# Group A's weighing in 512-column products, once in four steps, in an encoder block kernel

## The reference

```
sc = jnp.einsum('bqkgd,bskd->bkgqs', qblk, k, preferred_element_type=jnp.float32) * scale
p = jax.nn.softmax(sc, axis=-1).astype(v.dtype)
return jnp.einsum('bkgqs,bskd->bqkgd', p, v)
```

## Time and profile before

| | |
|---|---|
| median of 3 runs | 2183.95 us (2181.45 to 2187.36) |
| profiled execution | 2184.07 us |
| its span in the trace | 2182.3 us |
| PE, DVE, ACT, POOL busy | 2109.1, 1536.6, 747.1, 326.3 us |
| mean granted clock of PE | 0.988 of full |
| group A's attention | about 337 to 600 us |
| group B's attention | about 600 to 750 us |

### The profile page before, as it was taken

How to read it: one execution, slowest core, us unless ns; L and a number is a source line. 1 busy time by engine, 2 the same in 40 slices (tenths; PEclk the granted TensorE clock), 3 DMA queues, 4 the chain that set the end, 5 groups by cost and what they waited for, 6 DMA issues and landing times.

```text
span 2182.3 us, 29405 instructions
## 1 busy us (share of the span) xinstructions
PE 2109.1 (97%) x10566; PEld 1706.9 (78%) x10566; DVE 1536.6 (70%) x1985; ACT 747.1 (34%) x1197; POOL 326.3 (15%) x202
## 2 busy tenths in 40 slices
PE   7999999999989999999999999999999999998996
PEld 5778887776777788888888888888888888876885
DVE  7898635777666766677777777777777677767546
ACT  6323114666666721322222221122222221145223
POOL 5222101000011144201001000001001000015101
PEclk9999999999999999999999999999999999998998
DMA  5224357101267330011001001010001001011103
GB/s 178 108 95 154 121 176 173 29 14 29 43 155 165 82 131 32 20 39 39 29 29 38 29 29 38 29 33 34 29 34 33 29 29 38 29 46 41 39 29 116
DMA packets 54459, 139.98 MB, mean 64 GB/s; under 512 B 23296, under 2 KB 23680, under 8 KB 54400
## 3 DMA queue, kind: packets, MB, share of 16 engines
q1 hardware_dynamic: 53536, 138.07, 20.9%
q10 hardware_dynamic: 864, 1.13, 0.1%
HBM read 107.72 MB, written 31.46 MB: 64 GB/s over the span
## 4 chain that ended last, share of the span: by engine, by line
PE 86%; DVE 6%; DMA 2%; ACT 2%; issue 2%; POOL 1%; SPq 1%; DVEq 0%; ACTq 0%; POOLq 0%
PE ps L306 24%; PE ps L308 23%; PE ps L307 23%; PE ps L1160 4%; PE ps L1131 3%; PE ps L1114 2%; PE ps L1115 2%; DMA KLB<-qkl 1%; PE ps L1177 1%; DVE qstd L711 1%; PE ps L1124 1%; PE ps L1097 1%; PE ps L1080 1%; PE ps L1145 1%; DVE NL L1978 1%
## 5 line engine op out<-in xcount | busy, mean ns | idle before, releaser
L306 PE MATMUL ps<-NH,WH 128*128 128x512 f32 x1896 | 746.0, 393 | 21.2 <-DVE WL L694 10.0
L307 PE MATMUL ps<-NL,WH 128*128 128x512 f32 x1896 | 741.8, 391 | 0.0
L308 PE MATMUL ps<-NH,WL 128*128 128x512 f32 x1896 | 741.3, 391 | 0.0
L306 PEld LDWEIGHTS ps<-NH,WH 128*128 128x128 f32 x1896 | 358.3, 189 | 102.9 <-DVE NL L688 16.3
L308 PEld LDWEIGHTS ps<-NH,WL 128*128 128x128 f32 x1896 | 358.4, 189 | 75.3
L307 PEld LDWEIGHTS ps<-NL,WH 128*128 128x128 f32 x1896 | 358.6, 189 | 73.6
L1912 DVE TENSOR_TENSOR H<-H,ps 128x512 f32<-128x512 f32 x480 | 305.5, 684 | 100.9 <-PE ps L308 100.9
L283 POOL TENSOR_TENSOR raw<-raw,gains 128x1024 f32<-128x1024 f32 x76 | 154.2, 2031 | 1164.8 <-DMA raw<-in_w 1164.8
L298 ACT ACTIVATE WH<-raw 128x1024 fp32r<-128x1024 f32 x102 | 107.8, 1057 | 563.7 <-PE ps L308 536.0
L306 PE MATMUL ps<-MH,WH 128*128 128x512 f32 x504 | 196.6, 390 | 0.0
L307 PE MATMUL ps<-ML,WH 128*128 128x512 f32 x504 | 196.4, 390 | 0.0
(11 more groups left out here) (188 smaller groups left out, 2424.5 us busy)
## 6 DMA issues: line engine op xcount, KB each, us to landing
raw<-in_w SPq DMA_DIRECT2D x102, 512.0 KB, 3.3
xst<-in_xT SPq DMA_DIRECT2D x24, 256.0 KB, 3.3
H<-in_xT SPq DMA_DIRECT2D x8, 768.0 KB, 10.0
out_yT<-H SPq DMA_DIRECT2D x24, 256.0 KB, 2.1
Q<-qkh SPq DMA_DIRECT2D x12, 384.0 KB, 6.7
qkh<-oqh SPq DMA_DIRECT2D x5, 768.0 KB, 3.3
qkl<-oql SPq DMA_DIRECT2D x5, 768.0 KB, 4.9
qkh<-obh SPq DMA_DIRECT2D x5, 768.0 KB, 4.8
```

What stands on the lines that cost most here:

```text
L306: nc.tensor.matmul(out, wh, xh, start=first, stop=False)
L307: nc.tensor.matmul(out, wh, xl, start=False, stop=False)
L308: return nc.tensor.matmul(out, wl, xh, start=False, stop=last)
```

## The change

`weigh` of group A is now called once a block, at m = 4b+5, for all four items: 4 or 8 matmuls of 512 columns in place of twice as many of 256. The call at m = 4b+3 is gone, and with it PE goes from the transposes of that step straight to `norm_row`. The waits of `weigh` stay (`t_free` of item 4b+3, `o_sum` of the block before). `PA` has two slots of 512 queries, 32 KB, taken by `(m // 4 + 1) % 2`. `VF` and `PF` move within the region that they share with `PA`, and `VF`'s blocks lie in reverse order. No instruction of DVE, ACT, POOL or SP is added, removed or moved.

```
-        PA = c("PA", [2, TS // P, 2 * P])
-        PF = nc.alloc_sbuf_tensor_at("PF", [P, 2, 3, 2 * P], F32, offset=probs_home)
-        lows_home = c.at
-        VF = c("VF", [VBLOCKS, len(NA_LEFT), P])
-        c = Region(lows_home + 16 * KB)
+        PA = c("PA", [2, TS // P, GT])
+        VF = nc.alloc_sbuf_tensor_at("VF", [P, VBLOCKS, len(NA_LEFT), P], F32, offset=probs_home + 14 * KB)
+        PF = nc.alloc_sbuf_tensor_at("PF", [P, 2, 3, 2 * P], F32, offset=probs_home + 26 * KB)
...
-            return t[:, (m // 2) % 2, n0 * b:n0 * b + n, cols(m % 2, P)]
+            return t[:, (m // 4 + 1) % 2, n0 * b:n0 * b + n, cols(m % 4, P)]
...
-            return flat(VF[:, block, :, :]), ps[:, VBANK, :]
+            return flat(VF[:, VBLOCKS - 1 - block, :, :]), ps[:, VBANK, :]
...
-            def weigh(kind, p, b, m, queries):
+            def weigh(p, b):
 
                 s = b // 3
-                k0, w = window(kind, m)
-                at = (m % 4) * P
-                pe.wait_ge(t_free[0], fills(kind, p, ("T", m + queries // P - 1)) + T_FREE)
-                pe.wait_ge(t_free[1], fills(kind, p, ("T", m + queries // P - 1)) + T_FREE)
+                m = 4 * b
+                k0, w = window("A", m)
+                for half in range(2):
+                    pe.wait_ge(t_free[half], fills("A", p, ("T", m + 3)) + T_FREE)
                 at_least(pe, o_sum, p * 6 + b)
                 todo = places(w)
-                c0 = (m % 2) * P
                 for kb, kn, n in todo:
-                    mm = nc.tensor.matmul(ps[cols(kb % 2, DH), PVBANK, at:at + queries], VA[s][0:kn, k0 // P + kb, :],
-                                          PA[0:kn, (m // 2) % 2, n, c0:c0 + queries],
+                    mm = nc.tensor.matmul(ps[cols(kb % 2, DH), PVBANK, :], VA[s][0:kn, k0 // P + kb, :], PA[0:kn, (b + 1) % 2, n, :],
                                           start=kb < 2, stop=kb >= todo[-1][0] - 1)
-                return mm
+                mm.then_inc(pv_done, 1)
...
-                if kind == "A" and m % 2 == 1:
-                    mm = weigh(kind, p, (m - 3) // 4, m - 3, 2 * P)
-                    if m % 4 == 1:
-                        mm.then_inc(pv_done, 1)
+                if kind == "A" and m % 4 == 1:
+                    weigh(p, (m - 5) // 4)
```

More of the change, by code:

```diff
@@ L1176, in weigh_both @@
                     for half in range(2):
-                        mm = nc.tensor.matmul(ps[cols(half, DH), PVBANK_B[b % 2], cols((m // 2) % 2, P)], VF[0:kn, first + kb, (m + half) % 4, cols(s, DH)],
+                        mm = nc.tensor.matmul(ps[cols(half, DH), PVBANK_B[b % 2], cols((m // 2) % 2, P)], VF[0:kn, VBLOCKS - 1 - (first + kb), (m + half) % 4, cols(s, DH)],
                                               PF[0:kn, (m // 2) % 2, kb, cols(half, P)],
```

## The result

The changed kernel takes 2204.82 us (median of 4 runs, 2202.45 to 2205.66) against 2184.4 in the same comparison: a ratio of 1.0093, 95% interval 1.008 to 1.0106, or 20.4 us more. Its profiled execution has a span of 2202.2 us. The loss lies where the change is. Windows of the changed kernel (stretch, its length, busy us of each engine, clock, DMA): two laps of twelve steps, then the whole stage of group A.

A forecast was written before the change was run, and what follows sets the result against it. The prediction took PE to bound the kernel now, and after the change a ring over PE, DVE and ACT; 2184.1 + 14.1 (eight laps) + 2 (squares) = 2200 us, range 2188 to 2210, with 0.8.

The forecast's parts named there:

- Term 1: PE's bursts in group A: fewer, wider products, a sample burst 3.62 us, a prompt one 1.89, saving 0 to 7.4.
- The estimate of 8 us: PE's bursts: about 60 cycles of overhead per matmul, so 320 records fewer at 25 ns save 8 us, ending at 2192.
- gain of 7.4 us for entries and exits: PE's bursts: one entry (0.17 us) and one exit (0.14) fewer in each of 24 blocks.
- Term 2: PE's wait for DVE's `osum`, with weight loads, goes in group A: 6.7 us at most.
- the ring: Group A: exposed chain over PE, DVE and ACT from one burst's start to the next; +14.1 us, chance 0.76.
- Term 3: Group A: the dropped burst covered DVE's extra 1.50 us; without it a lap takes 33.25 us against 31.49, +14.1 in all.
- The three rings: One lap: sample burst with prompt copy 12.43 us; prompt burst, else samples 10.96; sample burst with prompt scores 9.86.
- Term 4: ACT's queue: squares between an exponential and a copy that PE waits for; 2 us taken, bounds 0 and 6.6.
- A: Attention stage of group A: PE stays the bound, the burst and `osum` gains count, 14.1 us less, 2170 us; chance 0.08.
- B: Group A: gains and losses cancel within 0.3%, 8 to 12 of the 16 us go, 2188 us; chance 0.08.
- C: PE's clock drops through idle pieces of up to 1 us, mean 0.9, 2215 us; chance 0.06.
- D: PE's two column halves no longer run side by side at 512 columns, 70 us more, 2270 us; chance 0.02.

The follow-up runs named there:

- narrow_once: Changed kernel with its one burst in step 4b+5 made of 256-column products again, two sets one behind the other: 2202.7 us, ratio 1.009.
- the wide kernel: Changed kernel with DVE's sum and product two steps later and POOL's first group B bias table ahead of the last pair's first addition: 2179.53 us, ratio 0.998.
- the narrow one: Kernel before, 256-column bursts kept, with DVE's product at the end of step 4b+7, norm rows at 4b+6 and POOL's table moved: 2177.91 us, ratio 0.9969.
- norm_later: Changed kernel with group A's norm rows one step later, behind the transposes of step 4b+4: 2205.19 us, ratio 1.0098.
- wide_small: Changed kernel with DVE's sum of the two halves made for only 8 of 512 columns, so its output is wrong: 2189.15 us, 15.7 less.
- narrow_small: Kernel before with DVE's sum of the two halves made for only 8 of 512 columns, so its output is wrong: 2175.76 us, 8.5 less.
- wide_late: Changed kernel with DVE's sum and product two steps later, end of step 4b+8, norm rows at 4b+7, squares behind the product: 2182.59 us, ratio 0.9997.
- wide_squares: Changed kernel with ACT's squares of group A beside a burst, ahead of the copy of the upper half: 2201.1 us, ratio 1.0094.

## Why the prediction was right

The forecast was 2200, the range 2188 to 2210, the measured time 2204.82. Step by step:

- Term 1, the burst. Forecast: 3.62 us for a sample block, 1.89 for a prompt one. The trace: 3.59 (468.05 to 471.64) and 1.87 (388.76 to 390.63), and twice as many records of half the width take 3.60 in `narrow_once`. The estimate of 8 us from the Trainium skill, "TensorEngine Tiling (Array Packing)", section "Instruction Overhead", finds no support here: 32 records or 16, the time of the burst is one. The estimate also took each record for a matmul; a product leaves two records, so that 160 products went, and by the same figure of the page the estimate would be 4 us.
- Its gain of 7.4 us for entries and exits is shown by no run. PE's busy time in 24 steps went from 61.47 to 61.36 us; with cover it is 60.04 in the wide kernel and 60.70 in the narrow one, 0.66 less, or 2.6 in the stage. None of it shortens a lap: even with cover the wide kernel has the narrow one's (61.31 and 61.22), with PE idle 1.27 us of it where the narrow one has 0.52. The forecast took nothing off for this gain, so the error did no harm.
- Term 2. The wait for `osum` went, as said, and was worth nothing, since it was inside the ring.
- Term 3, the ring, is borne out by four runs: `norm_later` (no single wait), `wide_small` and `narrow_small` (the same work exposed or half covered), `wide_late` (cover given back, loss gone). Its size was put too low: 33.25 us a lap against 34.05 measured. The three rings were forecast at 12.43, 10.96 and 9.86 us. By the starts of the bursts, 388.76, 399.96, 410.61, 423.38, 434.39, 444.50 and 456.86, they took 12.57, 11.11 and 10.38 on average. The first two are within the 0.25 that I allowed a ring; the third is not. One term failed in it in every lap, "row minimum to copy 0.60": it was read from a step whose copied item is a prompt one, and here the copy waits for eight transposes of a sample item, 472.40 to 473.28, 0.88 us. In the lap without squares that is nearly the whole error: its third ring took 10.11 us and its three rings 33.48, 0.23 above the forecast. The lap of the second head took 34.62, 1.37 above. 0.35 of it are squares (34.27 in `wide_squares`). Most of the rest goes with the longer hand-overs at DVE in that head's read-outs: copy to reciprocal 0.72, reciprocal to sum 0.20 and product to row minimum 0.72, against 0.61, 0.08 and 0.60 in the other lap. The sum of the earlier trace rows was read from a read-out of the first head alone and stood for all.
- Term 3 said that a burst hid DVE's extra 1.50 us before the change. It hid only a part: `narrow_small` shows that about half of the sum was on the path. The forecast did not suffer from it, since it set the ring against the measured lap, in which that part is contained.
- Term 4, the squares: 2 us taken, 1.4 measured. One is to be seen in the chain above, between the exponential's end and a copy: the scores started 0.05 us after the exponential, but the transposes had to wait until 478.10 for the copy behind the square.
- So 16.1 us were forecast and 20.4 came. The laps account for it: 14.1 forecast for eight of them, 8 x 0.80 = 6.4 more measured, together 20.5; the squares, for which I had put 2 us apart, are already in these laps. So the mechanism and the sign were right, and the size was four fifths of what came. The forecast's own range has a slip: with the ring's 6 us and the upper end of term 4 it reaches to 2211, not 2209; the measured time lies inside either.
- The rivals. A (PE stays the bound, 2170) and B (2188) were wrong. PE was idle 6.74 of 68.10 us, 10%, where I had 12%. C: the granted clock was 1.00 in the laps and 0.99 in the stage, as before, with idle pieces of up to 1.4 us at L1143; the rule of the Trainium skill, "TensorE: Matmul & The Clock Gate", section "A second HAM failure mode: psum-queue depth-cycling", did not come into play here. D: the bursts streamed at their old pace.

## What to carry to other kernels

An instruction on the engine that bounds is also the cover of what other engines do meanwhile. Before two bursts are merged into one, follow the queue of the engine that waits for them, from the end of one burst to the start of the next, and add up the chain; if it is longer than what is left on the bounding engine, the merger costs the difference. And the largest wait in the table need not be a bound: removing it may only move the idle time to the next link. To gain, move the work on the late engine, here a sum and a product, to just before or beside the burst, and look at what else waits in the queues that the move passes.

## What the runs showed of the hardware

That 16 records of 512 columns and 32 of 256 take the same 3.59 and 3.60 us, with 64 columns of weights in two halves side by side, was not expected to be so exact. Nor was it that DVE's starts follow each other by 0.20 and 0.72 us in the read-outs of the second head and by 0.08 and 0.60 in those of the first, in both kernels, for a cause that stays open, nor that 28.75 us of PE idle in short pieces, in a stage of 283, would leave its granted clock at the 0.99 that it had before.
